# Hybrid pooling, short-conv and ConvFFN step: 21 of 34 block turns moved from TensorE to transposing DMAs

## What is computed

```python
def _layer(x, ...):
    h = _rmsnorm(x, norm_mix)
    proj = h @ w_in                          # 1024 -> u | gb | gc | v, 512 each
    d, new_pool = _multi_scale_pool(u, prev_pool, start_pos)   # trailing means over 2/4/8/16, minus the token
    a = einsum('btgc,gcd->btgd', d, w_pool) * pool_scale
    conv, new_conv = _causal_dwconv(gc * v, prev_conv, conv_w)
    b = gb * conv
    x = x + concatenate([a, b]) @ w_out
    h = _rmsnorm(x, norm_ffn)
    up = h @ w_up                            # 1024 -> 5632
    upc, new_ffn = _causal_dwconv(up, prev_ffn, ffn_conv_w)
    val, gate = split(upc + ffn_conv_b)
    return x + (silu(gate) * val) @ w_down, new_pool, new_conv, new_ffn
def _rmsnorm(x, g):
    return x * rsqrt(mean(x * x) + 1e-6) * g
```

## Time and profile before

| | |
|---|---|
| median of 3 runs | 729.06 us (727.63 to 729.09) |
| profiled execution, its own time | 727.98 us |
| its span, slowest core | 726.4 us (cores 723.5 to 726.4) |
| PE matmul busy | 687.1 us, 95% |
| DVE / ACT / POOL busy | 502.0 / 336.1 / 225.1 us |
| mean granted TensorE clock, by core | 0.981 to 0.988 |
| DMA moved | 98.81 MB, mean 136 GB/s |

### The profile page before, as it was taken

How to read it: one execution, slowest core, us unless ns; L and a number is a source line. 1 busy time by engine, 2 the same in 40 slices (tenths; PEclk the granted TensorE clock), 3 DMA queues, 4 the chain that set the end, 5 groups by cost and what they waited for, 6 DMA issues and landing times.

```text
span 726.4 us, 12811 instructions; the slowest of 8 cores (723.5 to 726.4 us)
## 1 busy us (share of the span) xinstructions
PE 687.1 (95%) x3796; PEld 334.5 (46%) x3796; DVE 502.0 (69%) x860; ACT 336.1 (46%) x795; POOL 225.1 (31%) x422
## 2 busy tenths in 40 slices
PE   5969988879989999999999999999999999999996
PEld 4534454445534455444444444444444444444442
DVE  3486759988776456778778566787777276888724
ACT  4323357667623322766643233766630234666521
POOL 3173039777610000354431000444420001443300
PEclk7989999999999999999999999999999999999999
DMA  8989978999999565699999430899987222980002
GB/s 199 190 151 204 181 107 125 207 152 147 191 181 190 143 172 99 123 175 170 174 151 160 151 116 1 153 176 169 158 148 127 98 76 27 176 149 1 3 29 88
DMA packets 27894, 98.81 MB, mean 136 GB/s; under 512 B 3486, under 2 KB 3870, under 8 KB 27826
## 3 DMA queue, kind: packets, MB, share of 16 engines
q0 software_dynamic: 19440, 70.79, 61.2%
q1 hardware_dynamic: 8242, 26.95, 11.3%
q10 hardware_dynamic: 144, 0.26, 0.1%
HBM read 158.75 MB, written 10.01 MB: 232 GB/s over the span
## 4 chain that ended last, share of the span: by engine, by line
PE 82%; DMA 5%; DVE 5%; issue 5%; ACT 2%; POOL 1%; SPq 0%; DVEq 0%; ACTq 0%; POOLq 0%
PE G L544 50%; PE G L827 13%; PE G L828 13%; DMA wslot<-w_str 3%; PE TR L503 2%; DMA x1b<-xp 2%; PE G L1067 1%; DVE sm_arena L1012 1%; PE TR L544 1%; PE G L781 1%; PE G L782 1%; DVE arena L919 1%; DVE arena L928 1%; DVE arena L699 1%; ACT arena L890 0%
## 5 line engine op out<-in xcount | busy, mean ns | idle before, releaser
L890 ACT ACTIVATE arena<-G,cst_sb 128x512 f32<-128x512 f32 x176 | 134.9, 775 | 89.4 <-PE G L544 88.8
L544 PE MATMUL G<-aT,wslot 128*128 128x512 bf16 (+2 forms) x752 | 164.7, 376 | 2.8 <-DVE rs_all L467 1.9
L919 DVE SCALAR_TENSOR_TENSOR arena<-G,cst_sb,arena 128x512 f32<-128x512 f32 x176 | 124.0, 747 | 44.3 <-ACT Esave L895 43.3
L544 PE MATMUL G<-aT,sm_arena 128*128 128x512 bf16 x672 | 146.3, 379 | 0.0
L928 DVE SCALAR_TENSOR_TENSOR arena<-G,cst_sb,arena 128x512 f32<-128x512 f32 x176 | 125.5, 745 | 4.9 <-DVE OFp L926 0.5
L827 PE MATMUL G<-w_down_sb,actT 128*128 128x512 bf16 x330 | 125.1, 379 | 0.0
L828 PE MATMUL G<-w_down_sb,actT 128*128 128x512 bf16 x330 | 125.1, 379 | 0.0
L899 POOL TENSOR_TENSOR actT<-arena 128x512 bf16<-128x512 f32 x88 | 95.5, 1085 | 71.5 <-ACT arena L897 53.9
L544 PEld LDWEIGHTS G<-aT,wslot 128*128 128x128 bf16 x752 | 72.0, 98 | 85.4 <-issue 5.2
L544 PEld LDWEIGHTS G<-aT,sm_arena 128*128 128x128 bf16 x672 | 65.8, 98 | 79.3
L544 PE MATMUL G<-hT,wslot 128*128 128x512 bf16 (+1 forms) x400 | 89.6, 385 | 11.1 <-DVE sm_arena L616 3.4
(11 more groups left out here) (141 smaller groups left out, 682.6 us busy)
## 6 DMA issues: line engine op xcount, KB each, us to landing
wslot<-w_str POOLq DMA_DIRECT2D x70, 512.0 KB, 9.0
sm_arena<-w_str POOLq DMA_DIRECT2D x50, 512.0 KB, 9.0
x1b<-xp SPq DMA_DIRECT2D x13, 512.0 KB, 5.7
xrot<-xp SPq DMA_DIRECT2D x12, 512.0 KB, 12.5
yp<-x1b SPq DMA_DIRECT2D x12, 512.0 KB, 2.8
w_down_sb<-w_down POOLq DMA_DIRECT2D x11, 512.0 KB, 13.4
w_out_sb<-w_out POOLq DMA_DIRECT2D x4, 512.0 KB, 14.2
sm_arena<-xp SPq DMA_DIRECT2D x3, 512.0 KB, 3.7
```

Source lines behind the costliest of these rows:

```text
L544: ins = e.matmul(out_ap, lhsT=wslot[slot][:, k, half * 128:(half + 1) * 128], rhs=rhsT[:, k, c0:c0 + ncols], start=(k == 0), stop=(k == nk ...
L890: P.op("act", lambda e, tp=tp, g=g, c=c, h=h: e.activation(out=tp[:, h, 2:514], in_=G[g][:, :], func=AF.Identity, scale=cc(C_FW + 3 * c), ...
L919: P.op("dve", lambda e, g=g, c=c, h=h: e.scalar_tensor_tensor(out=tp[:, h, 1:513], in0=G[g][:, :], scalar=cc(C_FW + 3 * c + 1), in1=tp[:, ...
```

## The change

`norm_transpose` gets a switch `dma`. With it the turn is one DMA with transposition from hbuf straight to the block's columns of hT or aT (128 partitions by 8 by 128, bf16), issued by SP, and then the same multiply by DVE, now in place in hT or aT. It is set for all first norms of tiles 1 to 3 (12 turns) and for blocks 0 to 2 of the second norms of tiles 1 to 3 (9 turns). Tile 0, the 84 rows and the last block of each out projection stay with PE: 13 turns.

```diff
-        def norm_transpose(src, nrows, srckeys, hb, hk, dstT, col0, gcol, dstkeys, power=False):
+        def norm_transpose(src, nrows, srckeys, hb, hk, dstT, col0, gcol, dstkeys, power=False, dma=False):
...
+            def turn_dma():
+                dst = dstT[:, :, col0:col0 + 128]
+                P.op("sp", lambda e: e.dma_start_transpose(out=dst, in_=hb[:, :]), reads=[hk], writes=dstkeys,
+                     dsem=f"D_turn{HKI[hk]}")
+                P.op("dve", lambda e: e.tensor_tensor(
+                    out=dst, in0=dst, in1=cst_sb[:, gcol:gcol + 8].unsqueeze(2).to_broadcast([128, 8, 128]), op=ALU.mult),
+                    reads=["cst"], writes=dstkeys)
+                if hk in HKI:
+                    hfree.append(HKI[hk])
+
             def turn():
+                if dma:
+                    turn_dma()
+                    return
...
-            return norm_transpose(src, 128, [sk], hb, hk, hT, i * 128, C_G1, [("hT", i)], power)
+            return norm_transpose(src, 128, [sk], hb, hk, hT, i * 128, C_G1, [("hT", i)], power, dma=(s >= 1))
...
-            return norm_transpose(x1[r], 128, [("x1", r)], hb, hk, aT, i * 128, C_G2, [("aT", k, i) for k in range(8)])
+            return norm_transpose(x1[r], 128, [("x1", r)], hb, hk, aT, i * 128, C_G2, [("aT", k, i) for k in range(8)],
+                                  dma=(s >= 1 and i < 3))
```

## The result

| | before | changed |
|---|---|---|
| median of 4 runs each, same chip | 728.61 us (727.63 to 729.09) | 791.62 us (788.65 to 797.04) |
| ratio | | **1.087, 95% interval 1.081 to 1.094** |
| profiled execution: its time, its span | 727.98, 726.4 us | 788.65, 787.1 us |

The change costs 63 us, where 28 had been forecast: slower as forecast and inside the range, but more than twice the loss. Runs on different chips are compared by their ratios to the kernel before on the same chip.

The account below looks back on a forecast made before the run. PE was taken to bound the kernel, busy 687 of 726.4 us. Windows at +11.4, +18.1 and -1.35 and tile 0's stage 3 at 0 sum to +28.1 on 729.06, so 757 us, range 733 to 805.

Parts of the forecast that it names:

- The mechanism in the windows: First two windows: DVE's multiply waits for DMAs queued on SP, PE for the residual add behind; +11.4 and +18.1 us.
- T: Time from a turning DMA's issue to landing: 4.3 us for hT, 5.0 for the first two in the first window.
- tile 0's stage 3: Stretch before the windows: DVE waits some 9.5 us, offset by removed turns and shorter PE waits; 0, bounds -1.8 and +8.
- The upper bound of 5.7: High bound on T in us, taken from the landing of the first window's x load.
- Rival 3: Tile 0's stage 3 pays too: four waits reach PE at 7 us each, +28 on top, 785; chance 0.06.
- The chain of two aT landings: Window's end, after S, when PE may begin the last down projection block: 6.65 + 2Ta us, never under 11.8.
- Ta: Landing time of an aT turning DMA, with nothing queued ahead: 3.1 us, the middle of 2.4 and 3.8.
- The clock at 0: PE's granted clock in the windows, with new pauses: 0 cost, at most 5% of 2 x 65 us.
- The third window: No hT turns there; the aT chain is hidden and three turns are gained, -1.35 us (at 5.7: +1.7).
- the multiply: DVE's multiply from SBUF costed as before, 1.15 us; at 0.75 us it would give back 4 us.
- Rivals 1 and 2: 1: each 128x128 block costs, T = 10, 861 us, chance 0.14. 2: PE's shorter list decides, faster, chance 0.06.
- Rival 2: PE's shorter list decides: T near 1 us, or more slack in SP's loop, giving up to 719.6 us; chance 0.06.

## Why the prediction was right in sign and half in size

**The mechanism in the windows: right.** DVE's multiply waits for a DMA that stands on SP behind a load that waits for a store, and PE waits for the residual add behind it. The loop measured 11.37 + T, and early issue turned the loss of the windows into the full gain of their turns. The forecast is 32.7 us short: 11.6 in tile 0's stage 3, 16.0 in the first window, 4.9 in the second.

**The term that failed there: T.** I took one T from bytes (4.3, behind a load; 5.0 twice in the first window) and the measured ones are 7.52, 4.62, 4.77, 5.02 in the second window, sum 21.9 instead of 17.2, and 8.07, 7.76, 4.70, 7.30 in the first, sum 27.8 instead of 18.6. Put into the forecast's own formulas they give +22.2 for the second window (with aT's 2.8), where +23.0 was measured, and +24.3 for the first, where +27.4 was measured; of the rest, 2.2 is one y store that landed in 5.8 instead of 3.6. The upper bound of 5.7, a 512 KB load's landing, was no bound: four of the eight were above it. I had let half the bytes land a little after the load ahead of them, at 4.3; the medians are 7.5 behind loads of 6.7 in the first window and 4.9 behind loads of 4.4 in the second, and with the load moved behind it T fell to 3.7.

**Tile 0's stage 3: 0 was wrong, +11.6.** I gave the DMA the 12.5 us of the loads there; the first took 20.66, and DVE waited 17.7 us for it, not 9.5. The sum counted this wait as covered by PE's banks. It reached PE as one wait of 14.2, the one behind L942, so that only 3.5 were covered. PE's waits for weights, which were to shrink from 6.3, grew to 10.7 (6.4 and 4.3). Against that, 5.4 us of waits around the turns (3.3 and 2.1) and 1.8 of turns went. And the experiments show a second cost that the forecast didn't have at all: such a DMA can also delay the weights, by which the four cost 21 us even when nobody waits for them. In the changed kernel itself this hardly shows, as the longest landing of a weight DMA from 100 to 200 us is 12.2 there; a likely reason is that PE, held up by DVE, asks for them later. Rival 3, tile 0's stage 3 pays too, came true with 11.6 instead of its 28, in a forecast that gave it 0.06; to hold it apart from the main case was the error, since the DMA share of 0.96 there spoke for it.

**The chain of two aT landings: right, and a gain.** 6.65 + 2Ta with Ta = 2.82 is 12.3; from the end of the residual add (L803, 498.01) to stage 3 (510.89) the second window took 12.9. With PE turning these blocks, behind the same late hT turns, that way was 4.8 us longer. In the first window Ta was up to 7.15.

**The clock at 0: small, but not nothing.** PE's granted clock fell to 0.91 in both windows, and while PE waits for DVE that costs nothing. Behind a wait it does: at the end of the first window a turn and eight matmuls at half speed (0.57 from 324 to 328 us) took 1.9 us more. The +11.6 has 1.7 of the kind in it (the last 64 matmuls of tile 1's stage 1 took 15.68 us on this core, for 13.97), but one core of the kernel before shows that too. **The third window and the multiply:** -1.35 forecast, -1.2 measured (the window gained 1.34, the stage 3 ahead of it took 0.16 more); 1225 ns per multiply as costed, not 750.

**Rivals 1 and 2.** T never reached 10 in the windows; alone it is 2.8 for eight blocks. The Trainium skill, "VectorE: DVE Perf Modes", section "The three transpose paths", with its 1309 ns for one block of 128x128, would have made an estimated 10.5; the trace disagrees for eight blocks in one DMA. The Trainium skill, "Advanced Engine Details and Errata", section "X-Bar Transpose (TRN2)", calls transposing DMAs as fast as regular ones: the trace agrees when nothing else moves (2.8, beside 2.4 for a plain store of 256 KB), and disagrees in the full weight stream, 19.2 against 9.8 us. Rival 2 asked for more slack on SP's loop than there was; issued at the scale, it exists, and 14 turns bring 5.0 us.

## What to carry to other kernels

A DMA that takes work off the bounding engine has to be issued as soon as its source is ready: here the same DMAs cost 50 us in the first two windows when issued behind a store and a load, and gained 7.6 over the three windows when issued at the scale. Ask of each moved step which transfers run beside it, not only how many bytes it has: keep transposing DMAs out of a stretch where weights stream and PE lives on them, and leave those steps on PE. And where a DMA of a new kind is priced from rows of another kind, the landing of a plain DMA is no upper bound; where one stretch has other neighbours than the rest, it needs a case of its own.

## What the runs showed of the hardware

- A transposing DMA of 256 KB (bf16, eight blocks of 128x128 from SBUF to SBUF) lands in 2.8 us alone, 3.7 behind a store, 4.6 to 5.0 behind a 512 KB load, 6 to 9 beside weights, and in the full weight stream in a median of 12 to 19 and at longest 21 to 31. It makes 1056 packets of some 250 B.
- It can slow other queues: beside four of them in the weight stream two weight DMAs took 19.2 and 23.5 us (13.4 at longest before), and the kernel lost 21 us. The same bytes as plain copies cost 0; as plain copies into 256 B pieces 6, through a buffer that was read for longer and not through the weights.
- Its issue holds SP's sequencer for 1.22 us against 0.33 for a plain one, and for up to 12.4 us in the full stretch. The twelve of hT in the changed kernel (ns, min/median/max, then first and last start):

```profile
L498 SPq DMA_TRANSPOSE hT<-hbuf x12: 1217/1244/12407, 124.9 to 490.5; - x12
```

- Cores differ: with the four unread transposing DMAs the spans of the eight cores are 724.4 to 751.1 us, with 2 KB copies 722.6 to 726.4. The metric takes the worst core, so such a DMA costs more in it than in the mean.
- After a wait of 8.7 us PE ran a turn in 1.01 us and matmuls in 0.43 us for a while, about twice their time, at a granted clock of 0.66.
